# Decoder layer on one core: threshold steps with constants in PSUM, key and query transposes inside the last recurrence unit, two scans moved ahead of the attention

## Chip, core and metric

One Trainium2 chip, one core. The metric is the device time of one execution in microseconds (us), lower is better. TensorE is called PE, VectorE DVE, ScalarE ACT, GpSimd POOL, SyncE SP.

## What is computed

One layer of a hybrid decoder over 1024 prompt tokens and 8 decode tokens (1032 columns in all), width 1024, in fp32 accuracy (every matmul operand is split into a high and a low part). Of the reference, what matters here:

```
h   = modulate(rms_norm(x), shift, scale)
xr, gr, q, k, v, iq, ik, iw = split(h @ w_in)
xc  = causal_conv(xr);  r, gi = sigmoid(block products of xc)
a   = exp(-8 * softplus(-lambda) * r)
h_t = a_t * h_(t-1) + sqrt(1 - a_t^2) * gi_t * xc_t        (linear recurrence, 512 channels)
out_a = gelu(gr) * h
score = sum_heads iw * relu(iq . ik);  keep the 256 best keys of each query
out_b = softmax(q . k over the kept keys) @ v              (8 query heads, 2 key heads)
x = x + g1 * ([norm(out_a), norm(out_b)] @ w_out);  x = x + g2 * swiglu(...)
```

The 256 best keys are found without a sort: a search over the 32 bits of the score's float pattern gives each query its threshold (the 256th best score), then ties at the threshold are cut to the right number.

## The kernel before

The program is written by hand for each engine: every engine has its own instruction list and they meet at semaphores. Nothing is scheduled automatically; what stands first in an engine's list runs first. There are seven query groups with a search (`NSEL` = 7: six tiles of 128 prompt queries, with 384 to 1024 keys, and the 8 decode queries with 1025 keys).

**The search** runs 32 rounds. In each, DVE counts in four groups how many scores reach a candidate (L1974), ACT does the other three (L1282), and DVE sets the next bit (L2033). Candidates and bit constants lie in PSUM bank 7 (`raised`, `flips`, `limit`), so that the small steps of a round read one operand in PSUM. Meanwhile PE makes the projections and the units 0 to 5 of the recurrence inputs (`unit`, 72 matmuls of 344 columns each), and POOL rotates queries and keys, splits weights and runs the convolution.

**Behind the search** DVE finishes the last convolution group (`conv_last`, L2040) and then does the last threshold steps (L2065 to L2101): from the bit pattern found it makes the next larger pattern, counts once more for three groups (L1974), picks one of the two, and clears patterns near zero. All of these are operations on [128, 7] int32 tiles with a drain between dependent ones. Then come seven more counts, the number of ties to keep (L2110), and the tie steps of the first four groups (`ties(0)` to `ties(3)`, four operations each, L2122 to L1781). Between them stand the DVE parts of the recurrence gates: `gated(c)` (L2052), `root_input(c)`, `rooted(c)` (L2061) for its four channel groups c, and `ada_row_late` (L2007), which copies a row of modulation products out of PSUM.

**ACT** makes the gates: `gate_r`, `gate_i` (L1320, L1324), tanh, exp, square and `root` (L1335) for groups 0 and 1, then evacuates unit 6, waits for the semaphore `s_gx` to reach 5 (which is `rooted(1)`), and makes the gates of groups 2 and 3. **PE** makes `gate_products` (L2946) for each group into banks that ACT frees, then unit 7 (L2939 to L2941) into banks 0 to 2, which waits for ACT's seventh gate. Half-way through unit 7, `ada_columns_late` (L2924) and `ada_late` (L2918) make modulation products.

**The attention** then starts: `keys_turned(i)` (L2999, 16 matmuls) transposes two tiles of keys into PSUM bank 7 or 6, ACT and DVE split them into high and low (`keys_high` L1376, `keys_low` L2141); `q_transposed(n)` (L3009, 4 matmuls) does so for the queries of group n, from a stack that `q_high`, `q_low` (L1391, L2179) make. Its 16 groups n (8 tiles of queries times 2 key heads) go through a loop: `logits` on PE (L3022, L3023), `masked` on DVE (L2196), `exponential` on ACT (L1405), `scaled_probs` on DVE (L2207), `transposed` (L3032), `probs_out` on ACT (L1414) and `mixed` on PE (L3044). Logits and exponentials run two groups ahead (`AHEAD` = 2). The four `scan(c)` of the recurrence (L2165 to L2172) stand in DVE's list of this loop behind groups 3, 5, 7 and 9:

```
SCAN_AT = (3, 5, 7, 9)
                if n in SCAN_AT:
                    scan(SCAN_AT.index(n))
```

Behind the attention come the decode queries, the output projection and the feed-forward part.

## Time and profile before

| what | value |
|---|---|
| three runs | 1353.51 us median, 1352.86 to 1359.51 |
| profiled execution | 1357.33 us, its span 1355.5 us |
| busy share | PE 95%, PE weight load 86%, DVE 66%, ACT 50%, POOL 52% |
| chain that ended last | PE 65%, DVE 13%, SP queue 5%, ACT 4%, issue 4%, POOL queue 3% |
| mean granted PE clock | 0.970 of full |

Positions below are microseconds from the span's start. The search runs from 133 to 282, the last threshold steps from 291 to 308, unit 7 from 330 to 345, the attention from 345 to 509, and from about 570 PE works nearly without a gap to the end. A row of the timeline has start, duration, engine, line, operation, output<-inputs, shapes and count, and in brackets how long the engine had been idle and what released it. A chain row has start, duration, engine, what it writes and its line.

### The profile page before, as it was taken

Reading aid. Unit: us, or ns where it says so; the run is one execution under the profiler, and the core shown is the slowest. Engines: PE = TensorE matmul, PEld = TensorE weight load, DVE = VectorE, ACT = ScalarE, POOL = GpSimd, SP = SyncE. Lnnn points to the kernel's source line nnn. Section 1 sums busy time; section 2 is a strip of 40 time slices with the busy share of each in tenths; the row PEclk is TensorE's granted clock in tenths of the full one; section 3 lists DMA queues with packets and bytes.
Section 4 is the critical chain, followed back from the end, with each engine's and each line's share of the span. In section 5 each row is a group of like instructions: output and inputs, shape, how many; then the busy total and the mean of one; then the engine's idle time right before and its main releaser. Section 6 shows DMA issues by size and latency. Waiting matters only on the chain.

```text
span 1355.5 us, 25270 instructions
## 1 busy us (share of the span) xinstructions
PE 1289.2 (95%) x9473; PEld 1163.5 (86%) x9473; DVE 891.7 (66%) x1621; ACT 679.6 (50%) x1156; POOL 698.2 (52%) x439
## 2 busy tenths in 40 slices
PE   6889999999889998899999999999999999999998
PEld 4575998787746655699999999999999999999998
DVE  6766889888789844766895355554555544654495
ACT  5546978958767764545534333433433336311115
POOL 0331567990000000345578788887887867666730
PEclk9789999999789997999999999999999999999999
DMA  9622105443101114265522243343433457899733
GB/s 358 248 67 70 48 1 187 141 164 101 46 18 33 53 33 145 85 216 167 168 74 70 88 143 122 143 161 145 165 125 117 165 219 272 319 325 354 263 126 126
DMA packets 126058, 198.86 MB, mean 147 GB/s; under 512 B 16775, under 2 KB 100047, under 8 KB 115568
## 3 DMA queue, kind: packets, MB, share of 16 engines
q1 hardware_dynamic: 125936, 197.24, 42.0%
q8 instruction: 75, 1.23, 0.4%
q14 instruction: 47, 0.39, 0.1%
HBM read 144.07 MB, written 53.18 MB: 146 GB/s over the span
## 4 chain that ended last, share of the span: by engine, by line
PE 65%; DVE 13%; SPq 5%; ACT 4%; issue 4%; POOLq 3%; DVEq 3%; POOL 2%; ACTq 1%; DMA 0%
PE ps L3300 29%; PE ps L3320 14%; DVE junk L1974 2%; PE ps L3164 2%; PE ps L3044 2%; PE ps L3166 2%; PE ps L3165 2%; SPq L676 2%; PE ps L3032 1%; SPq L675 1%; DVE lg L2196 1%; PE ps L3097 1%; PE ps L3022 1%; SPq L670 1%; DVEq L2495 1%
## 5 line engine op out<-in xcount | busy, mean ns | idle before, releaser
L983 POOL TENSOR_TENSOR wL<-wraw,wH 128x1024 fp32r<-128x1024 f32 x28 | 69.5, 2484 | 297.0 <-ACT wH L1275 296.8
L3320 PE MATMUL ps<-input,down_H 128*128 128x258 f32 x1120 | 180.6, 283 | 1.5 <-DVE acc L2643 1.5
L3320 PEld LDWEIGHTS ps<-input,down_H 128*128 128x128 f32 x1120 | 154.5, 190 | 2.1 <-issue 1.1
L3300 PE MATMUL ps<-comb,opH 128*128 128x258 f32 x960 | 154.4, 283 | 0.0
L1106 POOL TENSOR_TENSOR opL<-wsum,opH 128x512 fp32r<-128x512 f32 x80 | 124.5, 1566 | 36.0 <-ACT opH L1604 32.8
L1604 ACT CAST opH<-wsum 128x512 fp32r<-128x512 f32 x80 | 49.6, 621 | 167.1 <-PE ps L3300 103.5
L3300 PEld LDWEIGHTS ps<-comb,opH 128*128 128x128 f32 x960 | 132.7, 190 | 0.0
L3300 PE MATMUL ps<-h2H,opH 128*128 128x258 f32 x640 | 129.0, 283 | 0.3 <-DVE h2L L2500 0.3
L3300 PE MATMUL ps<-h2H,opL 128*128 128x258 f32 x640 | 129.0, 283 | 0.0
L3300 PE MATMUL ps<-h2L,opH 128*128 128x258 f32 x640 | 128.6, 282 | 0.0
L2643 DVE TENSOR_TENSOR acc<-ps,acc 128x516 f32<-128x516 f32 x112 | 76.6, 694 | 62.2 <-PE ps L3320 61.7
L1282 ACT ACTIVATE junk<-score,keyX 128x896 bf16<-128x896 f32 (+2 forms) x96 | 106.0, 1106 | 18.5 <-DVE keyX L2033 14.0
L3320 PE MATMUL ps<-input,down_L 128*128 128x258 f32 x560 | 113.1, 283 | 0.0
L1106 POOL TENSOR_TENSOR opL<-raw,opH 128x512 fp32r<-128x512 f32 x60 | 94.1, 1569 | 33.5 <-ACT opH L1604 33.5
L1974 DVE TENSOR_SCALAR_CACHE_REDUCE junk<-score,keyX 128x384 bf16<-128x384 f32 (+5 forms) x138 | 106.3, 826 | 0.1
L3300 PEld LDWEIGHTS ps<-h2H,opH 128*128 128x128 f32 x640 | 99.3, 189 | 0.5 <-issue 0.5
L3300 PEld LDWEIGHTS ps<-h2L,opH 128*128 128x128 f32 x640 | 99.1, 189 | 0.0
L3300 PEld LDWEIGHTS ps<-h2H,opL 128*128 128x128 f32 x640 | 99.0, 189 | 0.0
L3300 PE MATMUL ps<-comb,opL 128*128 128x258 f32 x480 | 96.8, 283 | 0.0
L3320 PEld LDWEIGHTS ps<-input,down_L 128*128 128x128 f32 x560 | 86.7, 190 | 0.0
L2572 DVE TENSOR_TENSOR staged<-gf,staged 128x1032 fp32r<-128x1032 f32 x35 | 60.2, 1721 | 34.0 <-ACT staged L1636 34.0
L3300 PEld LDWEIGHTS ps<-comb,opL 128*128 128x128 f32 x480 | 74.2, 189 | 0.0
(506 smaller groups left out, 3518.9 us busy)
## 6 DMA issues: line engine op xcount, KB each, us to landing
down_inputs<-staged SPq DMA_DIRECT2D x35, 1032.0 KB, 4.5
input<-down_inputs SPq DMA_DIRECT2D x35, 1032.0 KB, 6.8
adb<-in_ada_w SPq DMA_DIRECT2D x8, 2048.0 KB, 8.4
wraw<-in_w_out SPq DMA_DIRECT2D x24, 512.0 KB, 4.5
raw<-in_w_gate SPq DMA_DIRECT2D x10, 1024.0 KB, 6.4
raw<-in_w_up SPq DMA_DIRECT2D x10, 1024.0 KB, 5.1
down_block<-in_w_down SPq DMA_DIRECT2D x5, 2048.0 KB, 10.9
x_feature_major<-x0T SPq DMA_DIRECT2D x1, 4128.0 KB, 12.0
```

Source lines behind the costliest of these rows:

```text
L676: sp.dma_start(ipg[b // 2][:, g, (b % 2) * HD:(b % 2 + 1) * HD], a["cache_ik"][0][bass.ds(page, 1), :, :].rearrange("a s d -> (a s) d")).t ...
L983: pool.tensor_tensor(lo[:], raw_[:], hi[:].bitcast(F32), ALU.subtract).then_inc(s_wL, 1)
L1106: pool.tensor_tensor(opL[g % OPS][:], operand(v, p), opH[g % OPS][:].bitcast(F32), ALU.subtract).then_inc(s_wL, 1)
L1282: ins = A(junk[0:m, off:off + w], score[0:m, off:off + w], ACT.Sign, scale=-1.0, bias=keyXs[r % 2][0:m, n:n + 1].bitcast(F32), accum_out=c ...
L1604: nc.scalar.copy(opH[g % OPS][:], operand(v, p)).then_inc(s_wH, 1)
L1974: V.tensor_scalar(junk[0:m, off:off + w], score[0:m, off:off + w], thr[0:m, n:n + 1].bitcast(F32), 0.0, op, ALU.add, accum_out=cnt[0:m, n: ...
L2572: V.tensor_tensor(stg[n % 2][:, :, 1, :], down_input(b, p), stg[n % 2][:, :, 0, :].bitcast(F32), ALU.subtract).then_inc(s_aL, 1)
L2643: V.tensor_tensor(two(acc[p][:, m, :]), ps[:, 2 * m:2 * m + 2, 0:HC], two(acc[p][:, m, :]), ALU.add).then_inc(s_dne, 1)
L3044: ins = mm(ps[par * HD:(par + 1) * HD, 6 + n % 2, 0:2 * P], value, heads[:, par], start=(k == 0), stop=(k == tile_of(n)))
L3164: mm(dst, wH[s][:, k, :], hi, start=(k == 0), stop=False)
L3300: ins = mm(ps[:, sum_bank(v, p) + h, 0:HC], weight[s][:, k, :], token[:, k, h * HC:(h + 1) * HC], start=begins, stop=ends, skip_group_chec ...
L3320: ins = mm(ps[:, 2 * m + h, 0:HC], weight[:, f, cc], tok[:, f, part, h * HC:(h + 1) * HC], start=(f == 0 and weight is hi and part == 0), ...
```

## The change

It has three parts.

1. **Constants in PSUM.** Nine int32 constants are set with `memset` and copied to bank 7 ahead of the search. The last threshold steps, which were `tensor_scalar` with immediates, become `tensor_tensor` whose second operand is such a constant, broadcast over the seven columns, or an intermediate kept in PSUM (`key_mask`, `key_carry`, `key_low`, `key_next`). `top_mask` and the XOR behind it become `pattern`. The seven counts then stand in one piece ahead of `gated(0)`.
2. **Attention transposes in unit 7.** `keys_turned(0)`, `(1)`, `(2)` and `q_transposed(0)` are issued between the feature blocks 4 to 7 of unit 7; `keys_turned(1)` writes bank 5 and `(3)` bank 6. ACT's `keys_high` and `q_high(0)` move ahead of `root(2)`.
3. **Two scans earlier.** `scan(0)` and `scan(1)` leave the attention loop and stand among the ties and gates; the loop keeps `scan(2)` behind group 5 and `scan(3)` behind group 9. `ties(1)` and `ties(2)` move ahead of `rooted(0)`.

The core of the diff:

```diff
 UNIT_BIT = (20, 22, 25, 28, 31, 32, 32, 32)
-SCAN_AT = (3, 5, 7, 9)
+SCAN_AT = {5: 2, 9: 3}
+KEY_BANK = (7, 5, 7, 6)
+F_TOPK = 0x43800000
+KEY_CONSTS = (31, 16, 1, 65535, -1, -2147483648, 0x7FFFFFFF, 1 << 23, F_TOPK)
...
+        key_mask, key_carry, key_low, key_next = [ps[:, 7, 320 + 8 * j:320 + 8 * j + NSEL].bitcast(I32) for j in range(4)]
...
-            root(2)
-            root(3)
...
-                if i == 0:
-                    act.wait_ge(s_qkr, 1)
-                else:
+                if i:
...
+            keys_high(0)
+            keys_high(1)
+            q_high(0)
+            root(2)
+            root(3)
+            keys_high(2)
+            q_evac(0)
             A(dsm[:, 7:8], consts[0:64, C_ONE:C_ONE + 1], ACT.Gelu_apprx_tanh)
-            act.wait_ge(s_un, NU_LRU)
-            q_high(0)
             unit_evac(7)
-            keys_high(0)
-            q_evac(0)
             q_evac(1)
-            keys_high(1)
+            keys_high(3)
             for g in range(GRP):
                 exponential(g)
-            keys_high(2)
             q_high(1)
             for g in range(GRP, AHEAD * GRP):
                 exponential(g)
-            keys_high(3)
             q_evac(AHEAD)
...
-            def top_mask(key):
-
-                V.tensor_scalar(keyM[:], key[:], 31, None, ALU.arith_shift_right)
+            def constant(value, n=NSEL):
+
+                at_ = 416 + KEY_CONSTS.index(value)
+                return ps[:, 7, at_:at_ + 1].bitcast(I32).to_broadcast([P, n])
+
+            def pattern(key):
+
+                V.tensor_tensor(keyM[:], key[:], constant(31), ALU.arith_shift_right)
+                V.tensor_tensor(keyN[:], key[:], constant(-1), ALU.bitwise_xor)
                 dve.drain()
-                V.tensor_scalar(keyM[:], keyM[:], -1, -2147483648, ALU.bitwise_xor, ALU.bitwise_or)
+                V.tensor_tensor(key_mask, keyM[:], constant(0x7FFFFFFF), ALU.bitwise_and)
                 dve.drain()
-
+                V.tensor_tensor(keyX[:], keyN[:], key_mask, ALU.bitwise_xor)
+                dve.drain()
+
+            for j, value in enumerate(KEY_CONSTS):
+                V.memset(kset[:, j:j + 1], value)
+            dve.drain()
+            V.tensor_copy(ps[:, 7, 416:416 + len(KEY_CONSTS)].bitcast(I32), kset[:])
             V.memset(negb[:], NEG)
...
-            V.tensor_scalar(keyM[:], keyX[:], 31, -2147483648, ALU.arith_shift_right, ALU.bitwise_or)
-            dve.drain()
-            V.tensor_tensor(keyK[:], keyX[:], keyM[:], ALU.bitwise_xor)
-            dve.drain()
-            V.tensor_scalar(keyL[:, 0, :], keyK[:], 65535, None, ALU.bitwise_and)
-            V.tensor_scalar(keyL[:, 1, :], keyK[:], 16, None, ALU.arith_shift_right)
-            dve.drain()
-            V.tensor_scalar(keyL[:, 0, :], keyL[:, 0, :], 1, None, ALU.add)
-            dve.drain()
-            V.tensor_scalar(keyN[:], keyL[:, 0, :], 16, None, ALU.arith_shift_right)
...
-            top_mask(keyC)
-            V.tensor_tensor(keyX[:], keyC[:], keyM[:], ALU.bitwise_xor)
-            dve.drain()
...
+            V.tensor_tensor(keyM[:], keyX[:], constant(31), ALU.arith_shift_right)
+            dve.drain()
+            V.tensor_tensor(key_mask, keyM[:], constant(-2147483648), ALU.bitwise_or)
+            dve.drain()
+            V.tensor_tensor(keyK[:], keyX[:], key_mask, ALU.bitwise_xor)
+            dve.drain()
+            V.tensor_tensor(keyL[:, 0, :], keyK[:], constant(65535), ALU.bitwise_and)
+            V.tensor_tensor(keyL[:, 1, :], keyK[:], constant(16), ALU.arith_shift_right)
+            dve.drain()
+            V.tensor_tensor(keyL[:, 0, :], keyL[:, 0, :], constant(1), ALU.add)
+            dve.drain()
+            V.tensor_tensor(key_carry, keyL[:, 0, :], constant(16), ALU.arith_shift_right)
+            V.tensor_tensor(key_low, keyL[:, 0, :], constant(65535), ALU.bitwise_and)
+            dve.drain()
+            V.tensor_tensor(keyL[:, 1, :], keyL[:, 1, :], key_carry, ALU.add)
+            dve.drain()
+            V.tensor_tensor(keyL[:, 1, :], keyL[:, 1, :], constant(16), ALU.logical_shift_left)
+            dve.drain()
+            V.tensor_tensor(keyC[:], keyL[:, 1, :], key_low, ALU.bitwise_or)
+            V.tensor_tensor(key_next, keyL[:, 1, :], key_low, ALU.bitwise_or)
+            dve.drain()
+            pattern(keyC)
             count(ALU.is_ge, keyX, SEL_ACT)
...
+            V.tensor_tensor(keep[:, SEL_ACT:], cnt[:, SEL_ACT:], constant(F_TOPK, NSEL - SEL_ACT).bitcast(F32), ALU.is_ge)
+            dve.drain()
+            V.copy_predicated(keyK[:, SEL_ACT:], keep[:, SEL_ACT:], key_next[:, SEL_ACT:])
+            dve.drain()
+            pattern(keyK)
+
+            V.tensor_tensor(keyN[:], keyX[:], constant(0x7FFFFFFF), ALU.bitwise_and)
+            V.memset(key_next, 0)
+            dve.drain()
+            V.tensor_tensor(keep[:], keyN[:], constant(1 << 23), ALU.is_lt)
+            dve.drain()
+            V.copy_predicated(keyX[:], keep[:], key_next)
             dve.drain()
             ada_row_late(ADA_1 + 5)
+            count(ALU.is_gt, keyX)
+            dve.drain()
+            V.tensor_scalar(cnt[:], cnt[:], -1.0, float(TOPK), ALU.mult, ALU.add)
+            dve.drain()
             gated(0)
-            count(ALU.is_gt, keyX, 0, SEL_ACT)
             gated(1)
-            count(ALU.is_gt, keyX, SEL_ACT)
-            dve.drain()
-
-            V.tensor_scalar(cnt[:], cnt[:], -1.0, float(TOPK), ALU.mult, ALU.add)
-            dve.drain()
-            root_input(0)
-            root_input(1)
...
-            ties(0)
-            rooted(0)
-            rooted(1)
-            ada_row_late(ADA_1 + 6)
-            ties(1)
-            gated(2)
-            gated(3)
-            ties(2)
-            root_input(2)
-            root_input(3)
-            ada_row_late(ADA_1 + 7)
-            ties(3)
...
+            ties(0)
+            ties(1)
+            root_input(0)
+            root_input(1)
+            ties(2)
+            rooted(0)
+            rooted(1)
+            ada_row_late(ADA_1 + 6)
+            dve.wait_ge(s_lev, 6)
+            scan(0)
+            gated(2)
+            gated(3)
+            ties(3)
+            root_input(2)
+            root_input(3)
+            ada_row_late(ADA_1 + 7)
+            keys_low(0)
+            keys_low(1)
             q_low(0)
-            keys_low(0)
+            scan(1)
+            keys_low(2)
             rooted(2)
...
-            keys_low(1)
+            keys_low(3)
             for g in range(GRP, AHEAD * GRP):
                 masked(g)
-            keys_low(2)
             q_low(1)
-            keys_low(3)
...
-                    scan(SCAN_AT.index(n))
+                    scan(SCAN_AT[n])
...
-                    if k == KH and between is not None:
-                        pe.wait_ge(s_gs, 2 * LT)
-                        ada_columns_late(between - 1, 3, 0)
-                        ada_late(between)
+                    if between is not None:
+                        between(k)
...
-            unit(7, hH, hL, 0, ADA_1 + 7)
 
             def keys_turned(i):
-                if i >= 2:
-                    pe.wait_ge(s_kl, i - 1)
+                if i == 2:
+                    pe.wait_ge(s_kl, 1)
...
-            pe.wait_ge(s_qkr, 1)
-            keys_turned(0)
+            def attention_begun(k):
+
+                if k == KH:
+                    pe.wait_ge(s_gs, 2 * LT)
+                    ada_columns_late(ADA - 2, 3, 0)
+                    ada_late(ADA - 1)
+                    pe.wait_ge(s_qkr, 1)
+                    keys_turned(0)
+                elif k == KH + 1:
+                    keys_turned(1)
+                elif k == KH + 2:
+                    keys_turned(2)
+                elif k == KD - 1:
+                    q_transposed(0)
+
+            unit(7, hH, hL, 0, attention_begun)
             ada_columns_late(ADA - 1, 6, 0)
-            pe.wait_ge(s_gs, 2 * LT)
-            q_transposed(0)
+            pe.wait_ge(s_kl, 2)
             q_transposed(1)
             pe.wait_ge(s_lmod, 1)
-            keys_turned(1)
+            keys_turned(3)
             pe.wait_ge(s_lev, NU_LRU)
-            pe.wait_ge(s_kl, 1)
-            for g in range(GRP):
+            for g in range(AHEAD * GRP):
                 logits(g)
-            keys_turned(2)
-            for g in range(GRP, AHEAD * GRP):
-                logits(g)
-            keys_turned(3)
             pe.wait_ge(s_kl, NTT // 2)```

What it does to DVE's list around the gates of groups 0 and 1 (spare and gel hold the gate terms, eqb and preb the tie terms, mrowb a modulation row; L1781 is the helper for three-operand steps, and L1783 in the new kernel). Before:

```order
L1781 SCALAR_TENSOR_TENSOR spare_174<-spare_173,spare_174 128x1032 [waits decay_squared]
L1781 SCALAR_TENSOR_TENSOR gel<-gel 128x1032 [waits decay_squared]
L2122 TENSOR_SCALAR eqb<-score,keyX 128x384
L2125 SCALAR_TENSOR_TENSOR preb<-eqb 128x384
L1781 SCALAR_TENSOR_TENSOR eqb<-preb,cnt,eqb 128x384
L1781 SCALAR_TENSOR_TENSOR score<-score,keyX,eqb 128x384
L2061 TENSOR_TENSOR xr<-xr,spare_174 128x1032 [waits lru_root]
L2061 TENSOR_TENSOR xr<-xr,gel 128x1032 [waits lru_root]
```

Now, in the same place:

```order
L1783 SCALAR_TENSOR_TENSOR spare_175<-spare_174,spare_175 128x1032 [waits decay_squared]
L1783 SCALAR_TENSOR_TENSOR gel<-gel 128x1032 [waits decay_squared]
L2131 TENSOR_SCALAR eqb<-score,keyX 128x640
L2134 SCALAR_TENSOR_TENSOR preb<-eqb 128x640
L1783 SCALAR_TENSOR_TENSOR eqb<-preb,cnt,eqb 128x640
L1783 SCALAR_TENSOR_TENSOR score<-score,keyX,eqb 128x640
L2075 TENSOR_TENSOR xr<-xr,spare_175 128x1032 [waits lru_root]
L2075 TENSOR_TENSOR xr<-xr,gel 128x1032 [waits lru_root]
L2021 COPY mrowb_148<-ps 128x256 [waits ada_columns,ada_product]
L2021 COPY mrowb_149<-ps 128x256
L2156 TENSOR_TENSOR decay_170<-decay_170,stT 128x8 [waits lru_evacuated]
L2157 SCALAR_TENSOR_TENSOR xr<-decay_170,xr 128x1024
```

The ties between the root inputs and the rooted products are now those of 640 keys; those of 384 and 512 keys stand ahead of the root inputs, and a scan follows the row copies.

On PE, behind unit 7, before (qk holds the keys to turn, stk the stacked queries):

```order
L2999 MATMUL ps<-consts,qk 64x128 [waits qk_rotated]
L2999 MATMUL ps<-consts,qk 64x128 x7
L2924 MATMUL ps<-consts,mrowb_147 128x9 [waits ada_row_evacuated]
L2924 MATMUL ps<-consts,mrowb_147 128x9
L2924 MATMUL ps<-consts,mrowb_148 128x9 x2
L3009 MATMUL ps<-consts,stk 128x128 [waits q_stack_low,gate_sigmoid]
L3009 MATMUL ps<-consts,stk 128x128 x3
L3009 MATMUL ps<-consts,stk 128x128 [waits q_stack_low]
L3009 MATMUL ps<-consts,stk 128x128 x3
L2999 MATMUL ps<-consts,qk 64x128 [waits late_modulation_ready]
L2999 MATMUL ps<-consts,qk 64x128 x7
L3022 MATMUL ps<-kT,qT 128x128 [waits bank_evacuated,k_low,lru_evacuated]
```

Now, from the end of unit 7 on:

```order
L2937 MATMUL ps<-consts,mrowb_148 128x9 [waits ada_row_evacuated]
L2937 MATMUL ps<-consts,mrowb_148 128x9
L2937 MATMUL ps<-consts,mrowb_149 128x9 x2
L3019 MATMUL ps<-consts,stk 128x128 [waits q_stack_low,k_low]
L3019 MATMUL ps<-consts,stk 128x128 x3
L3009 MATMUL ps<-consts,qk 64x128 [waits late_modulation_ready]
L3009 MATMUL ps<-consts,qk 64x128 x7
L3032 MATMUL ps<-kT,qT 128x128 [waits bank_evacuated,lru_evacuated]
```

One key transpose and one query transpose are left there; the others now stand inside unit 7, where the third of them waits for `k_low` and the query transpose for `q_stack_low`, both of which DVE gives.

## Rows read from the trace of the kernel before

**Rows 1.** The chain that ended last, 290 to 305 us: start, us, engine and what.
```profile
290.79 1.73 DVE keyM L2065
292.85 2.21 DVE keyL L2069
295.20 0.94 DVE keyL L2072
296.83 1.05 DVE keyL L2079
298.44 2.26 DVE keyM L1993
304.66 1.63 DVE keep L2088
```
**Rows 2.** Timeline of POOL over the same stretch.
```profile
290.06 2.43 POOL L1045 TENSOR_TENSOR gel<-gel 128x1032 f32<-128x1032 f32 x1 [0.15 <-issue]
...
295.01 2.84 POOL L1042 TENSOR_SCALAR gel<-xr,vec 128x1024 f32<-128x1024 f32 x1
...
298.29 2.38 POOL L1045 TENSOR_TENSOR gel<-gel 128x1032 f32<-128x1032 f32 x1
...
303.90 2.36 POOL L1051 TENSOR_TENSOR xr<-xr,gel 128x1032 f32<-128x1032 f32 x1
```
**Rows 3.** Timeline of DVE: a search step with PSUM operand, two later small steps.
```profile
278.16 0.16 DVE L1987 TENSOR_TENSOR keyX<-keyX,ps 128x7 int32<-128x7 int32 x1
...
297.95 0.17 DVE L2081 TENSOR_TENSOR keyC<-keyL 128x7 int32<-128x7 int32 x1
298.20 0.17 DVE L1991 TENSOR_SCALAR keyM<-keyC 128x7 int32<-128x7 int32 x1
```
**Rows 4.** The instructions of line 1926, the bit constants ahead of the search.
```profile
L1926 DVE MEMSET bits<- x31: 59/59/59, 73.2 to 75.2; 128x1 int32 x31
```
**Rows 5.** Timeline of DVE: the second rooted product.
```profile
324.75 1.23 DVE L2061 TENSOR_TENSOR xr<-xr,gel 128x1032 f32<-128x1032 f32 x1
```
**Rows 6.** Timeline of ACT: gate_i(1), and gate_r(2) behind its table load.
```profile
308.10 1.12 ACT L1324 ACTIVATE gel<-ps,vec 128x1032 f32<-128x1032 f32 x1 [0.62 <-PE ps L2946]
...
326.02 1.12 ACT L1320 ACTIVATE decay<-ps,vec 128x1032 f32<-128x1032 f32 x1
```
**Rows 7.** Stretches of ties(1), ties(2): length, busy of steps on score, clock.
```profile
326.77:330.33 3.56, 0.00 (x0) 0.00 (x0) 1.24 (x2) 0.00 (x0) 1.00 1.05 356
333.27:337.33 4.06, 0.00 (x0) 0.00 (x0) 1.43 (x2) 0.00 (x0) 1.00 0.02 4
```
**Rows 8.** Timeline of PE from unit 7's end to the first turned probabilities.
```profile
344.98 1.09 PE L2999 MATMUL ps<-consts,qk 128*64 128x128 f32 x16
...
353.35 1.98 PE L2999 MATMUL ps<-consts,qk 128*64 128x128 f32 x16
...
360.77 1.11 PE L3009 MATMUL ps<-consts,stk 128*128 128x128 f32 x4 [1.41 <-DVE kT L2141]
361.81 1.12 PE L3032 MATMUL ps<-consts,lg 128*128 128x128 f32 x4
```
**Rows 9.** The chain that ended last, at the first and third scan.
```profile
383.05 2.20 DVE xr L2166
...
387.06 1.15 DVE score L1781
...
419.72 2.20 DVE xr L2166
```
**Rows 10.** Timeline of PE behind the first scan.
```profile
389.47 0.50 PE L3022 MATMUL ps<-kT,qT 128*128 128x512 f32 x1 [2.12 <-DVE nb L2196]
```
**Rows 11.** Stretches: busy of PE, PE load, DVE, ACT, POOL; clock; DMA share; GB/s.
```profile
350.00:366.00 16.00, 14.27 (x82) 12.21 (x78) 9.83 (x43) 10.00 (x28) 0.00 (x0) 0.50 0.21 60
390.00:398.00 8.00, 7.13 (x25) 3.98 (x25) 6.26 (x18) 6.37 (x16) 0.00 (x0) 0.57 0.19 54
415.00:430.00 15.00, 13.05 (x86) 8.70 (x83) 14.53 (x32) 11.50 (x25) 0.00 (x0) 1.00 0.07 21
```

33 lines of the change are left out of this document (11 added, 22 removed).

## The prediction

> **What bounds the kernel now.** I read four views. The table of the page says that PE is busy 95% of the span and has 65% of the chain that ended last; DVE has 13% of it. From about 570 us to the end PE works nearly without a gap, so whatever lets the attention end earlier should bring the end forward by as much. The question is therefore which waits between 282 and 509 us the change takes from the chain, and the rest of the reading stays there.
>
> The chain [rows 1] shows six of DVE's last threshold steps with 0.94 to 2.26 us each, all on [128, 7] tiles. Small steps of the same shape take 0.17 us and start 0.25 us after one another when each waits for the one before [rows 3] (the two from 297.95 on). The timeline of POOL [rows 2] says what the long ones have in common: the first ends at 290.79 + 1.73 = 292.52, as POOL's step of 290.06 ends (292.49); the second ends at 295.06, where POOL's next but one starts (295.01); the fourth at 297.88, with POOL's scalar step (297.85); the fifth at 300.70, with 298.29 + 2.38 = 300.67; the sixth at 306.29, with 303.90 + 2.36 = 306.26. DVE waits for POOL in them. The Trainium skill, SBUF — State Buffer, "Who interferes with whom", says that a DVE instruction in a mode that uses both port pairs, or one with two SBUF inputs against a POOL step that reads SBUF, is blocked for POOL's whole instruction, and that one with a single SBUF input outside those modes is not; by that rule, which these five ends fit, the new steps would never wait.
>
> In the attention loop the chain runs through the scans [rows 9]; PE waits 2.12 us for DVE behind the first [rows 10], and the granted clock is 0.57 of full in the 8 us from 390 on, so mostly at 1.2 instead of 2.4 GHz [rows 11]. Around the third scan PE is busy 13.05 of 15 us and DVE 14.53 of 15 [rows 11].
>
> **The change part by part.**
>
> *Constants.* Nine memsets and a copy are added ahead of the search. The 62 memsets that alternate from 73.2 to 75.2 [rows 4] start 0.03 us apart and last 0.06, so nine are 0.3 to 0.5 us, and the copy behind a drain is one step of 0.25. Every engine's work follows the search's rounds there, so I take it in full: **+0.6** (0 to +0.8).
>
> *Threshold steps.* The six long ones sum to 9.82 us; at 0.17 each they would be 1.02, so 8.8 go. The new list has one more dependent step (0.25) and three more second halves of a pair (about 0.08 each), 0.5 in all: 8.3 us less. This assumes 0.16 us for a `tensor_tensor` with a PSUM operand, which the search shows 31 times on the same shape [rows 3] (278.16). The Trainium skill, VectorE: DVE Perf Modes, "The TRN2 errata", speaks against that: it gives 120 cycles of fixed cost for a PSUM source against 58 for SBUF at 0.96 GHz, which is an estimate of 65 ns more for each of some 25 steps, 1.6 us, and would make the forecast 1347.2. The row at 278.16 (PSUM) is not longer than the one at 297.95 (SBUF), so the measurement decides for 0.16.
>
> *Order before unit 7.* ACT's gates of groups 2 and 3 wait for `rooted(1)`, which ended at 324.75 + 1.23 = 325.98 [rows 5], and ACT went on at 326.02 [rows 6]; PE's unit 7 follows from them. Ahead of that point DVE now has `ties(1)` and `ties(2)` too, 3.56 and 4.06 us [rows 7], and `gated(1)`, behind all counts, may wait for ACT's gate, which ends at 308.10 + 1.12 = 309.2 [rows 6]; I reckon 0.4. So -8.3 + 3.56 + 4.06 + 0.4 = -0.3: all that the threshold steps give is spent on ties. An earlier `rooted(1)` brings little, since ACT has a table load right ahead of 326.02. Unit 7 starts as before: **0** (-0.3 to +1.1, if both `gated` steps wait).
>
> *Start of the attention.* Up to the loop DVE's list has two scans more (8.4, below) and 8.3 less, so DVE reaches its first `masked` as before. PE has the same transposes, but two of the 16-matmul groups that cost 1.98 at the low clock [rows 8] (353.35) are issued inside unit 7, where such a group takes 1.09 (344.98): 1.8 less; and the wait of 1.41 for the last keys at 360.77 [rows 8] should go, since `keys_low(2)` and `(3)` are earlier. If DVE alone sets the start, nothing is gained; if PE does, 3.2. Walking both lists with these durations I get the first turned probabilities at 359.8 instead of 361.81: **-2.0** (-3.2 to 0). What is late next there is DVE's `s_lmod`, for which PE's last key transpose waits behind `scan(1)` and `keys_low(2)`.
>
> Inside unit 7 PE can now block: `keys_turned(2)` waits for `keys_low(0)`, `q_transposed(0)` for `q_low(0)`, and 18 and 9 matmuls of unit 7 stand behind them. My walk has about 1.5 us of slack at both, so I cost the waits at nothing; that cover goes if DVE is later than that.
>
> *First scan out of the loop.* It begins one small step (0.17) before the chain's row of 383.05, and the next work starts at 387.06 [rows 9]: 4.2 us in which DVE gives nothing to PE and ACT. Below stands PE's recorded wait of 2.1 [rows 10]; above, 4.2 plus what the low clock costs in the 8 us from 390 (PE 7.13 busy at 0.57 [rows 11]), some 2 more that PE would not need. I take the scan and a little of the clock: **-4.5** (-6 to -2.1).
>
> *The scan behind group 7* (419.7 [rows 9]) is the second place that gets none; groups 5 and 9 keep theirs. Here the clock is full, and PE idles only 15 - 13.05 = 1.95 us [rows 11], so PE takes over as the bound once DVE is 4.2 shorter: **-2.0** (-4.2 to 0).
>
> The SP queue loads key pages of the decode queries behind `scan(0)` and `scan(1)`; these now go out earlier, and nothing waits for them before the loop ends. POOL is idle from 306.3 on. Both nothing.
>
> Sum: 0.6 - 2.0 - 4.5 - 2.0 = **-7.9**. Against the profiled execution's own 1357.33 us (span 1355.5, 1.8 outside it) that is 1349.4; this execution lies 3.8 above the median of the three runs, so against the median it is 1353.5 - 7.9 = **1345.6 us**.
>
> **The rivals.**
>
> *The loop is PE's already.* PE and ACT have enough other work in the loop, and the removed scans pay only what PE was seen to wait: 2.1, and 0.5 for the second. For it speaks PE's 13.05 of 15 us; against it the low clock behind the first scan, which a PE that is the bound would not show. -2.6 - 2.0 + 0.6 = -4.0: 1349.5.
>
> *The long steps are first uses, not waits for POOL.* Each long step of rows 1 uses an operation that DVE has not run before in that form, and a repetition is short. Then the new list pays again: it has nine pairs of operation and place (shift, and, or, add, left shift, less-than, with output in SBUF or PSUM) that the search does not run, each at the mean excess of 8.8 / 6 = 1.47, so 13.2 us. That delay reaches `rooted(1)`, unit 7 and the attention at once, less 0.3 of slack: 1345.6 + 12.9 = 1358.5, slower by 5.0. It decides against the change from 7.9 + 0.3 = 8.2 us on, some six of the nine. Against it: five ends agree with POOL's to 0.05 us, and the first `or` of two tensors, at 297.95, takes 0.17 [rows 3].
>
> *PE keeps its clock at the start.* From 350 to 366 us PE is busy 14.27 of 16 us at half clock [rows 11]. With the transposes inside unit 7, less idle time stands ahead of the logits; if the clock then does not fall, PE's 14.27 would be about 7.1, and ACT (10.0) and DVE (9.83) set the pace. Of the 6 us between I give it half, 3: 1342.6. Against it: PE still waits for DVE between unit 7 and the logits, as it did when the clock fell.
>
> **How the numbers follow.** Forecast 0.60, PE's loop 0.25, clock 0.09, first uses 0.06. All bounds of the terms at once give -13.5 and -0.2; the forecast's own range is 1341.5 to 1350, and with the rivals 1341.5 to 1351.5 leaves out no more than 2 in 10. A measurement of this kernel can tell about 0.5% from no change, 6.8 us: faster is under 1346.7, slower over 1360.3. The forecast lies under 1346.7 in four of five of its cases (0.48), the clock rival in all (0.09), PE's loop in few (0.03): 0.60. Slower takes the dearest first uses: 0.03. The rest, 0.37, is within.
>
> **What would show it.** In the profile of the changed kernel: the steps between `conv_last` and the seven counts have no row over 0.3 us beside POOL's rows and take about 9 us with three counts, not 17; if rows of 1 to 2 us stand there and end where no POOL row ends, the second rival holds. `rooted(1)` ends within 1 us of 326.6 (the old time plus 0.6) and unit 7 starts as late behind it as before. PE shows no wait for `kT` or `stk` inside unit 7. The first turned probabilities come near 360.4. There is one scan between 380 and 425 us, no stretch at half clock near 390, and the loop's 147 us (361.8 to 509) are about 140.5. The forecast is wrong if that loop is over 144 us (the first rival), or if PE idles inside unit 7.

## The result and the profile after

The changed kernel takes 1349.39 us in the median of 13 runs (1346.16 to 1354.34), the kernel before, in runs beside it, 1356.87 (1352.86 to 1361.23). The ratio is 0.9949, 95% interval 0.9937 to 0.9962: 6.9 us less (5.2 to 8.5), at the edge of the 0.5% that was called no change. The forecast was -7.9 with a range of -12.0 to -2.0, against 1353.5 us, the median of three earlier runs of the kernel before; the 1345.6 us that it named goes with that figure, so the differences are compared and not the times. The profiled execution of the changed kernel took 1351.9 us, span 1350.1.

Of the page's busy table and of its chain, after:

```profile
PE 1284.1 (95%) x9473; PEld 1161.0 (86%) x9473; DVE 882.8 (65%) x1635; ACT 679.3 (50%) x1156; POOL 698.7 (52%) x439
PE 71%; DVE 11%; SPq 5%; issue 3%; ACT 3%; DVEq 2%; POOLq 2%; POOL 1%; DMA 1%; ACTq 0%
```

DVE's share of the chain fell from 13 to 11%, PE's rose from 65 to 71%.

The two profiled executions are not aligned: the search ends (start of its last COPY_PREDICATED) at 281.80 us before and at 286.67 after. So I compare stretches, not positions. The modulation columns in unit 7 are PE's step half-way through that unit (`ada_columns_late`); the first turned probabilities are PE's first `transposed` step.

| stretch, us | before | after | change |
|---|---|---|---|
| start to end of the search | 281.80 | 286.67 | +4.87, of it 0.44 the constants |
| end of the search to the modulation columns in unit 7 | 54.61 | 54.21 | -0.40 |
| from there to the first turned probabilities | 25.40 | 21.75 | -3.65 |
| the attention loop, to PE's first step of the decode queries | 147.40 | 141.28 | -6.12 |
| from there to the end of the span | 846.3 | 846.2 | -0.1 |

The threshold steps, timeline of DVE after, to be held against [rows 1]:

```profile
295.33 0.16 DVE L2079 TENSOR_TENSOR keyM<-keyX,ps 128x7 int32<-128x7 int32 x1
...
298.10 0.17 DVE L2001 TENSOR_TENSOR ps<-keyM,ps 128x7 int32<-128x7 int32 x1
...
302.22 0.16 DVE L2103 TENSOR_TENSOR keep<-cnt,ps 128x3 int32<-128x3 f32 x1
...
304.33 0.76 DVE L2021 COPY mrowb<-ps 128x256 f32<-128x256 f32 x2
```

POOL's timeline beside them:

```profile
294.60 2.41 POOL L1050 TENSOR_TENSOR gel<-gel 128x1032 f32<-128x1032 f32 x1 [0.15 <-issue]
297.16 2.41 POOL L988 TENSOR_TENSOR lL<-lraw,lH 128x1024 fp32r<-128x1024 f32 x1
```

POOL works as before, and no small step is longer than 0.17 us. The block lasts 304.33 - 295.33 = 9.00 us, against 308.15 - 290.79 = 17.36 before.

What the saved time became stands in three timelines, of DVE, ACT and PE, after:

```profile
329.21 1.24 DVE L2075 TENSOR_TENSOR xr<-xr,gel 128x1032 f32<-128x1032 f32 x1
```
```profile
330.48 1.12 ACT L1325 ACTIVATE decay<-ps,vec 128x1032 f32<-128x1032 f32 x1 [0.80 <-DVE xr L2075]
```
```profile
331.65 3.74 PE L2957 MATMUL ps<-xr,wbd 128*128 128x344 f32 x12 [1.59 <-ACT decay L1325]
```

`rooted(1)` ends 43.8 us behind the search's end (330.45 - 286.67), where it ended 44.2 behind it [rows 5]. ACT could have gone on 0.80 us sooner.

The start of the attention, timeline of PE after, against [rows 8]:

```profile
343.61 1.09 PE L3009 MATMUL ps<-consts,qk 128*64 128x128 f32 x16
...
348.90 1.09 PE L3009 MATMUL ps<-consts,qk 128*64 128x128 f32 x16
...
351.46 0.60 PE L3019 MATMUL ps<-consts,stk 128*128 128x128 f32 x4
...
355.61 1.09 PE L3009 MATMUL ps<-consts,qk 128*64 128x128 f32 x16 [0.84 <-DVEq L2233]
356.63 0.33 PE L3032 MATMUL ps<-kT,qT 128*128 128x128 f32 x1
...
361.63 1.09 PE L3019 MATMUL ps<-consts,stk 128*128 128x128 f32 x4 [1.26 <-issue]
362.63 1.11 PE L3042 MATMUL ps<-consts,lg 128*128 128x128 f32 x4
```

Nothing inside unit 7 waits. Three key transposes and one query transpose that stood behind it are now in it at full clock, and the next thing late is DVE's `s_lmod` (L2233), 0.84 us. The query transpose ahead of the first turned probabilities, which waited 1.41 us for keys before, still waits 1.26, now for DVE's `q_low`, which ends at 360.84 + 0.69 = 361.53:

```profile
360.84 0.69 DVE L2170 TENSOR_TENSOR stk<-qk,stk 128x512 fp32r<-128x512 f32 x1
```

The stretch from the modulation columns to the first turned probabilities, before and after (columns as in [rows 11]):

```profile
336.41:361.81 25.40, 22.48 (x163) 18.45 (x161) 18.37 (x42) 19.09 (x39) 0.00 (x0) 0.76 0.12 35
340.88:362.63 21.75, 18.52 (x163) 14.88 (x161) 18.04 (x45) 18.66 (x39) 0.00 (x0) 0.96 0.07 20
```

PE has the same 163 matmuls there. They keep it busy 3.96 us less, at a mean clock of 0.96 instead of 0.76, and it waits 3.23 us (21.75 - 18.52) where it waited 2.92 (25.40 - 22.48). So all of the 3.65 us, and a little more, is work done at a higher clock; the waits did not get shorter.

Stretches after: length, busy of PE, PE load, DVE, ACT, POOL; clock; DMA share; GB/s, to be held against [rows 11]:

```profile
350.00:361.00 11.00, 8.41 (x66) 7.44 (x66) 9.36 (x29) 10.62 (x24) 0.00 (x0) 1.00 0.11 32
361.00:366.00 5.00, 4.37 (x20) 4.03 (x21) 3.21 (x16) 3.62 (x14) 0.00 (x0) 0.50 0.23 66
...
390.00:398.00 8.00, 6.44 (x40) 4.18 (x40) 6.47 (x18) 6.68 (x17) 0.00 (x0) 1.00 0.20 58
...
415.00:430.00 15.00, 13.96 (x92) 9.15 (x92) 11.14 (x25) 12.31 (x25) 0.00 (x0) 1.00 0.01 2
```

Before, PE was at half clock from 350 to 366; now it is so only from 361. The half-clock stretch near 390 is gone. Around 415 to 430 PE's busy time rose from 13.05 to 13.96 of 15 and DVE's fell from 14.53 to 11.14.

### The profile page after: what moved, and what is told of

It is laid out like the page before. It is cut to its first block, busy times and chain, and to the rows that moved or that the text cites. A ratio compares the mean times of both kernels' runs of the same rounds, so it can differ in the third digit from the quotient of the medians.

```text
span 1350.1 us, 25285 instructions
## 1 busy us (share of the span) xinstructions
PE 1284.1 (95%) x9473; PEld 1161.0 (86%) x9473; DVE 882.8 (65%) x1635; ACT 679.3 (50%) x1156; POOL 698.7 (52%) x439
## 3 DMA queue, kind: packets, MB, share of 16 engines
q8 instruction: 75, 1.23, 0.4%
## 4 chain that ended last, share of the span: by engine, by line
PE 71%; DVE 11%; SPq 5%; issue 3%; ACT 3%; DVEq 2%; POOLq 2%; POOL 1%; DMA 1%; ACTq 0%
PE ps L3318 29%; PE ps L3338 14%; PE ps L3054 2%; PE ps L3182 2%; PE ps L3183 2%; PE ps L3184 2%; SPq L681 2%; PE ps L2919 2%; PE ps L2921 2%; PE ps L3042 2%; PE ps L2920 1%; SPq L680 1%; DVE lg L2187 1%; PE ps L3115 1%; SPq L675 1%
## 5 line engine op out<-in xcount | busy, mean ns | idle before, releaser
L988 POOL TENSOR_TENSOR wL<-wraw,wH 128x1024 fp32r<-128x1024 f32 x28 | 69.5, 2485 | 286.9 <-ACT wH L1280 286.8
```

The source lines that it names most:

```text
L988: pool.tensor_tensor(lo[:], raw_[:], hi[:].bitcast(F32), ALU.subtract).then_inc(s_wL, 1)
```

## The experiments

All times are against the kernel before in the same session, from the ratio of medians times 1356.9 us, with the 95% interval. The other columns are read from one profiled execution of each kernel, with the marks of above: where the search ends, from there to the modulation columns in unit 7 and to the first turned probabilities, and the length of the loop. Single executions scatter: the four whose scans stand behind 3, 5, 7 and 9 (before, constants only, all scans back, forms warmed) have loops of 145.73 to 147.40 us, and the kernel before and the one with forms warmed, which has the same loop, differ by 1.67. In that pair the clock from 388 to 396 us is 0.66 and 0.79. The four with the changed kernel's two scans (changed, immediates, SBUF constants, ties(2) behind) lie closer, 141.18 to 141.55. A difference of 1 to 2 us between two loops below is therefore a reading of two executions and no more.

| kernel | time, us | ratio | search ends | to unit 7 | to attention | loop |
|---|---|---|---|---|---|---|
| before | 0 | 1 | 281.80 | 54.61 | 80.01 | 147.40 |
| changed | -6.9 (-8.5 to -5.2) | 0.9949 | 286.67 | 54.21 | 75.96 | 141.28 |
| constants only | -2.0 (-3.9 to -0.1) | 0.9985 | 281.41 | 53.47 | 77.50 | 146.95 |
| all scans back | -3.0 (-4.7 to -1.1) | 0.9978 | 283.15 | 53.61 | 75.04 | 147.02 |
| scan(1) behind 3 | -4.3 (-6.2 to -2.3) | 0.9968 | 286.96 | 54.24 | 75.66 | 145.10 |
| scan(1) behind 7 | -8.3 (-10.6 to -6.1) | 0.9939 | 285.19 | 53.60 | 75.02 | 142.64 |
| immediates | +1.1 (-0.5 to +2.7) | 1.0008 | 282.02 | 62.72 | 84.48 | 141.55 |
| SBUF constants | -4.3 (-6.2 to -2.6) | 0.9968 | 282.35 | 57.83 | 79.59 | 141.26 |
| scans behind 9, 12 | +7.6 (+5.2 to +9.9) | 1.0056 | 282.29 | 54.45 | 76.56 | 143.68 |
| scans behind 7, 10, 12 | +7.5 (+5.0 to +9.9) | 1.0055 | 283.04 | 54.21 | 75.63 | 144.55 |
| tie step moved | -5.8 (-7.9 to -3.8) | 0.9957 | 284.81 | 53.60 | 75.02 | 143.93 |
| scans behind 5, 7 | -9.1 (-11.3 to -6.9) | 0.9933 | 284.99 | 54.28 | 76.03 | 140.66 |
| ties(2) behind | -7.6 (-10.0 to -5.3) | 0.9944 | 281.27 | 53.57 | 75.34 | 141.18 |
| forms warmed | +1.2 (-0.5 to +3.0) | 1.0009 | 283.81 | 54.28 | 79.67 | 145.73 |

### The first part alone

The kernel before, with `keyM` to `keyX` as in the changed kernel's diff, the constants and `pattern`, but `gated`, counts, `ties`, scans and transposes where they were:

```diff
-            V.tensor_scalar(keyM[:], keyX[:], 31, -2147483648, ALU.arith_shift_right, ALU.bitwise_or)
+            V.tensor_tensor(keyM[:], keyX[:], constant(31), ALU.arith_shift_right)
+            dve.drain()
+            V.tensor_tensor(key_mask, keyM[:], constant(-2147483648), ALU.bitwise_or)
...
```

> The kernel before with the first part alone: constants and intermediates in PSUM, the order of all lists as before. Port theory (the long steps waited for POOL): no step over 0.3 us between the last convolution group and the seven counts, that stretch 8.3 us shorter; but ahead of unit 7 DVE was waited for only once, 0.92 us at ACT's first root, so unit 7 starts about 0.9 us earlier relative to the end of the search and the rest of the 8.3 becomes idle time of DVE; at the attention's start the wait of 1.4 us for the last keys may go too. Time: 0.6 - 0.9 - (0 to 1.4), 1 to 2 us under the kernel before, within what can be told from no change. First-use theory: long steps stay, slower by 0 to 5 us. If the whole 8.3 us were on the path, the time would fall by 7 to 8 us.

Measured -2.0 us. Unit 7's columns come 1.14 us sooner, the attention 2.51. The 0.92 us that ACT waited for DVE's root input is in ACT's timeline of before:

```profile
319.39 1.06 ACT L1335 ACTIVATE spare<-spare 128x1032 f32<-128x1032 f32 x1 [0.92 <-DVE spare L1781]
```

So 8.4 us off DVE's list, with nothing put in their place, are worth about a quarter of that. From the search's end to unit 7's columns ACT of this run has no wait for DVE over 0.15 us left, only waits for PE, so the chain of ACT's gates and PE's products sets the pace there. The wait for the last keys at the attention's start, which I thought might go, stays at 1.41 us. The 1.37 us gained behind the columns (24.03 against 25.40) come with a clock of 0.87 instead of 0.76: PE is busy 20.06 us instead of 22.48 and waits 3.97 instead of 2.92.

### The scans

Three kernels from the changed one: all four back in the loop, `scan(1)` alone back behind group 3, and the same behind group 7.

```diff
-SCAN_AT = {5: 2, 9: 3}
+SCAN_AT = {3: 0, 5: 1, 7: 2, 9: 3}
...
-            dve.wait_ge(s_lev, 6)
-            scan(0)
...
-            scan(1)
```
```diff
-SCAN_AT = {5: 2, 9: 3}
+SCAN_AT = {3: 1, 5: 2, 9: 3}
...
-            scan(1)
```
```diff
-SCAN_AT = {5: 2, 9: 3}
+SCAN_AT = {5: 1, 7: 2, 9: 3}
...
-            scan(1)
```

> The changed kernel with all four scans back in the attention loop behind groups 3, 5, 7 and 9 (parts 1 and 2 stay). Theory of the prediction: the two scans pay 6.5 us in the loop, so the time is 6 to 7 us over the changed kernel, less what DVE gains ahead of the attention without them (at most 1 to 2 us, since DVE is waited for there 0.84 us by the last key transpose): 4.5 to 6.5 us over it, and the clock falls again behind the first scan. Rival (the loop is PE's already): 2.6 us in the loop and the start earlier by 1 to 2, so 0.5 to 2 us over the changed kernel.

> The changed kernel with scan(1) back in the loop behind group 3; scans behind 5 and 9 stay. Theory: place 3 costs 4.5 us (2.1 if only PE's recorded wait counts), with a stretch at about half clock near 390 us; the start of the attention is up to 0.8 us earlier. So 1.3 to 4.5 us over the changed kernel, 3.7 likeliest.

> The changed kernel with scan(1) back in the loop behind group 7; scans behind 5 and 9 stay. Theory: place 7 costs 2.0 us (0 to 4.2) at full clock, the start of the attention is up to 0.8 us earlier: 1.2 us over the changed kernel, and less than with place 3. If every scan in the loop costs its 4.2 us wherever it stands, this one and the run with place 3 come out alike, 3.4 us over.

Measured -3.0, -4.3 and -8.3 us, so 3.9 and 2.6 over and 1.4 under the changed kernel by the medians. Only the first is apart from the changed kernel beyond the intervals (0.9965 to 0.9992 against 0.9937 to 0.9962); it is less than the 4.5 to 6.5 expected, and the third has the other sign than the 1.2 over that was expected. The loops go with the places: 147.02 with all four, 142.64 without place 3 (4.4 less), 141.28 without 7 too (1.4 less), and 145.10 with 3 but not 7 (3.8 over the changed kernel). The difference can be dated: `attT` of the fourth group (L2204) is copied 27.5 us behind the first turned probabilities with the scan at 3 and 23.3 without, and the gap stays to the loop's end. Both differences of the loop are near the forecast's 4.5 and 2.0, the second within the scatter of single executions. From 388 to 396 us the clock was 0.69 with the scan at 3 (all four back) and 1.00 without it (scan(1) behind 7). That the time with all scans back is 3.9 and not 6 to 7 over is in small part the start: the attention begins 0.92 us sooner (75.04 against 75.96). The run with scan(0) ahead and scan(1) not has 75.02, so scan(0) is free there. Of the 0.94 between that run and the changed kernel only 0.33 can be scan(1)'s: 0.61 lie ahead of the columns in unit 7 (53.60 against 54.21), where both lists are the same, and where `gated(1)` waits 0.45 us for ACT in the changed kernel's profile and not in the other. From the columns on it is 21.42 or 21.43 us in all five runs with scan(1) in the loop, and 21.75 to 21.77 in five of the six with it ahead (22.11 with scans behind 9 and 12). PE's timeline with scan(1) behind 7 shows what it held up:

```profile
352.61 1.09 PE L3008 MATMUL ps<-consts,qk 128*64 128x128 f32 x16
```

The last key transpose has no wait for `s_lmod` left; the query transpose behind the logits waits longer instead (1.93 us against 1.26), so little is gained. By the profiles `scan(1)` ahead of the attention costs 0.3 us and behind group 7 it costs 1.4; the times don't tell the two kernels apart (0.9922 to 0.9955 against 0.9937 to 0.9962).

### The immediates back

The changed kernel with the threshold steps of before, all else as changed (the `constant` and `pattern` of the diff reversed):

```diff
-            V.tensor_tensor(keyM[:], keyX[:], constant(31), ALU.arith_shift_right)
+            V.tensor_scalar(keyM[:], keyX[:], 31, -2147483648, ALU.arith_shift_right, ALU.bitwise_or)
...
```

> The changed kernel with the threshold steps of before again (immediates, no PSUM operands); the order of the lists, with ties(1) and ties(2) ahead of the rooted products, stays. Theory (port waits, and the 8.3 us were spent on the order ahead of unit 7): six or so steps of 1 to 2.3 us come back, that stretch is 17 us again, and now all of it reaches rooted(1), ACT's gates, unit 7 and the attention, less 0.8 us of slack at ACT: 7 to 8 us over the changed kernel, about as slow as or slower than before. If the saved 8.3 us had been idle time, the run would be within 1 us of the changed kernel.

Measured +1.1 us, 8.0 over the changed kernel; unit 7 and the attention start 8.5 us later, the loop is as long (141.55). The whole 8.4 us arrive. So the constants are worth 2 us in the old order and 8 in the new one, where two ties stand in the time they freed. ACT waits for DVE in this run at `gated(0)`, at the first root input and at `rooted(1)`:

```profile
317.33 1.07 ACT L1336 ACTIVATE spare<-decay 128x1032 f32<-128x1032 f32 x1 [3.52 <-DVE xr L2054]
...
326.15 1.06 ACT L1340 ACTIVATE spare<-spare 128x1032 f32<-128x1032 f32 x1 [5.30 <-DVE spare L1783]
...
333.99 1.12 ACT L1325 ACTIVATE decay<-ps,vec 128x1032 f32<-128x1032 f32 x1 [1.23 <-DVE xr L2063]
```

The changed kernel has only the third of these waits, 0.80 us.

### Why the steps were long

Two kernels. The changed one with its constants read from SBUF (the tile `psum_r` is unused there until the attention):

```diff
-                at_ = 416 + KEY_CONSTS.index(value)
-                return ps[:, 7, at_:at_ + 1].bitcast(I32).to_broadcast([P, n])
+                at_ = KEY_CONSTS.index(value)
+                return kset[:, at_:at_ + 1].to_broadcast([P, n])
...
+        kset = psum_r[:, 0:len(KEY_CONSTS)].bitcast(I32)
```

And the kernel before with the forms run once ahead of the search:

```diff
+            V.memset(keyC[:], 1)
+            dve.drain()
+            V.tensor_scalar(keyM[:], keyC[:], 31, -2147483648, ALU.arith_shift_right, ALU.bitwise_or)
+            V.tensor_scalar(keyL[:, 0, :], keyC[:], 65535, None, ALU.bitwise_and)
+            V.tensor_scalar(keyL[:, 1, :], keyC[:], 16, None, ALU.arith_shift_right)
...
```

> The changed kernel with the nine constants read from SBUF instead of PSUM, the same tensor_tensor steps otherwise; so some ten of them have two SBUF inputs while POOL works. Port theory: steps of 0.5 to 2.5 us appear in the threshold stretch and end where a row of POOL ends; the stretch is 12 to 18 us, the time 3 to 8 us over the changed kernel. If two SBUF inputs don't wait for POOL (only the immediates' form did), the stretch stays at 9 us and the time within 1 us of the changed kernel. First-use theory says nothing about the operand's place: 9 us too, since none of these steps was long in the changed kernel.

> The kernel before with the immediates' forms of the threshold steps run once on unused tiles ahead of the search (shift with or, and, shift, add, left shift, xor with or, less-than). Port theory: the six long steps stay as long as they were (0.9 to 2.3 us) and end where POOL's rows end; the time is up to 0.8 us over the kernel before. First-use theory: the forms are known by then, all steps of the stretch take 0.2 us, and the stretch is 8.8 us shorter.

Timelines of DVE and POOL with SBUF constants:

```profile
291.00 1.71 DVE L2079 TENSOR_TENSOR keyM<-keyX,psum_r 128x7 int32<-128x7 int32 x1
...
293.29 1.97 DVE L2085 TENSOR_TENSOR keyL<-keyK,psum_r 128x7 int32<-128x7 int32 x1
...
295.44 0.90 DVE L2088 CUSTOM_DVE_ANT_0 keyL<-psum_r,keyL 128x14 uint16<-128x14 uint16 x1
...
302.02 0.17 DVE L2103 TENSOR_TENSOR keep<-cnt,psum_r 128x3 int32<-128x3 f32 x1
...
303.31 0.17 DVE L2109 TENSOR_TENSOR keyN<-keyX,psum_r 128x7 int32<-128x7 int32 x1
```
```profile
290.27 2.42 POOL L1050 TENSOR_TENSOR gel<-gel 128x1032 f32<-128x1032 f32 x1 [0.15 <-issue]
292.84 2.40 POOL L988 TENSOR_TENSOR lL<-lraw,lH 128x1024 fp32r<-128x1024 f32 x1
295.21 2.85 POOL L1047 TENSOR_SCALAR gel<-xr,vec 128x1024 f32<-128x1024 f32 x1
...
301.06 2.91 POOL L1054 TENSOR_SCALAR xr<-xr,vec 128x1032 f32<-128x1032 f32 x1 [0.17 <-issue]
```

The first ends at 292.71, POOL's step at 292.69; the second at 295.26, POOL's at 295.24. One change of the second operand's place, PSUM to SBUF, turns 0.16 us into 1.71 and 1.97 in the same instruction. The stretch, up to the row copy at 304.17, is 13.17 us, 4.2 over the changed kernel's. The time is 2.6 over it, less than the 3 to 8 expected and with intervals that overlap (0.9954 to 0.9981 against 0.9937 to 0.9962). So what decides is whether the second operand lies in SBUF while POOL works; the form with immediates is not needed for the wait. The Trainium skill, SBUF — State Buffer, "Who interferes with whom", says that a DVE instruction with two SBUF inputs contends with a POOL instruction that reads SBUF. These two rows agree; those at 302.02 and 303.31, 0.17 us inside POOL's scalar step of 301.06 to 303.97, do not, nor do three more with two SBUF inputs during it and five during the one of 295.21, and the measurement decides: here tensor_tensor waited for POOL's tensor_tensor to its end, and during POOL's scalar steps it was long only once, 0.90 us at 295.44, with no end of POOL's there.

With the forms warmed, DVE and POOL:

```profile
292.42 1.72 DVE L2079 TENSOR_SCALAR keyM<-keyX 128x7 int32<-128x7 int32 x1
...
300.07 2.27 DVE L1993 TENSOR_SCALAR keyM<-keyM 128x7 int32<-128x7 int32 x1
```
```profile
291.69 2.42 POOL L1045 TENSOR_TENSOR gel<-gel 128x1032 f32<-128x1032 f32 x1 [0.15 <-issue]
...
299.92 2.39 POOL L1045 TENSOR_TENSOR gel<-gel 128x1032 f32<-128x1032 f32 x1
```

All six are as long as before to 0.01 us (1.72, 2.21, 0.94, 1.05, 2.27, 1.64), and the two shown end with POOL's rows (294.14 and 294.11; 302.34 and 302.31). The forms of the first five had run ahead of the search, 0.16 to 0.17 us each; that of the sixth, a comparison of counts, had not. For the five, first use has nothing to do with it; the sixth rests on its end alone, which agrees with POOL's to 0.03 us in the kernel before (306.29 and 306.26).

### Later places for the scans

DVE was busy 43 of the 50 us from 380 to 430 in the changed kernel (the expectation below has 45, misread), but only 50 of 79 from 430 on, so I tried the late groups:

```diff
-SCAN_AT = {5: 2, 9: 3}
+SCAN_AT = {9: 2, 12: 3}
```
```diff
-SCAN_AT = {5: 2, 9: 3}
+SCAN_AT = {7: 1, 10: 2, 12: 3}
...
-            scan(1)
```

> The changed kernel with the two scans that stay in the loop behind groups 9 and 12 instead of 5 and 9. In its trace DVE is busy 45 of the 50 us from 380 to 430 but only 50 of the 79 from 430 to 509. Theory that a scan costs by how full DVE is where it stands: the place behind group 5 costs 1 to 3 us, the late ones nothing, so 1 to 3 us under the changed kernel. Against: if the loop is PE's by then, within 0.5 us; if the last scan delays the key pages of the decode queries (the SP queue loads two of them behind the fourth scan), the decode stage grows instead.

> The changed kernel with scan(0) ahead of unit 7 as it is and the other three in the loop behind groups 7, 10 and 12. With scan(1) behind group 7 the time was 1.4 us under the changed kernel (start 0.9 us earlier, loop 1.4 us longer in the profiles). If a scan costs by how full DVE is where it stands, taking the place behind group 5 away too gives 2 to 4 us under the changed kernel in all. If not, 1 to 2.

Both misses: +7.6 and +7.5 us over the kernel before, 14.5 over the changed one. Two causes can be seen. The loop became 2.4 and 3.3 us longer instead of shorter. And the decode stage waits; SP, ACT and PE with scans behind 9 and 12:

```profile
538.71 2.57 SPq L714 DMA_DIRECT2D wraw<-in_w_out  x3
```
```profile
542.78 1.04 ACT L1280 CAST wH<-wraw 128x1024 fp32r<-128x1024 f32 x1 [8.15 <-DMA wraw<-in_w_out]
```
```profile
544.88 1.97 PE L3148 MATMUL ps<-consts,kpg 128*128 128x128 f32 x8 [6.66 <-ACT kbT L1464]
```

SP in the changed kernel:

```profile
525.86 2.47 SPq L714 DMA_DIRECT2D wraw<-in_w_out  x3
```

SP loads the key pages of two decode queries only when the fourth scan is done, then 48 value pages (52.9 us of its queue here), then these weights. The weights are asked for 12.9 us later, and ACT and PE wait for them. From the loop's end to the end of the span it is 7.8 and 9.6 us more. (With scans behind 9 and 12 the profile so shows 0.6 + 2.4 + 7.8 = 10.8 of the 14.5; that profiled execution lay 3.8 under its kernel's median, and the changed kernel's 2.5 over its own.) I had named the key pages as what could be late; it is the weights two places behind them in the same queue.

The loop taught the second thing. Per place, from the loops of these runs (a scan more or less, differences of the positions at which each group's `attT` is copied): 3.8 to 4.4 us behind group 3, 1.2 behind 5, 1.4 behind 7, about 2 behind 9, 3.0 behind 10, 2.1 and 3.6 behind 12 in the two runs. Behind 3, 10 and 12 a tie step stands behind the scan in the same group, behind 5, 7 and 9 none (`TIE_AT`). Each of these prices comes from one or two pairs of single executions.

### A tie step away from the scan

```diff
-SCAN_AT = {5: 2, 9: 3}
+SCAN_AT = {3: 1, 5: 2, 9: 3}
...
-TIE_AT = ((0, 1, 2, 3), (4, 6, 8, 10), (11, 12, 13, 14))
+TIE_AT = ((0, 1, 2, 4), (4, 6, 8, 10), (11, 12, 13, 14))
...
-            scan(1)
```

> The run with scan(1) behind group 3, with the last tie step of the fifth group moved from group 3 to group 4, where the scan no longer stands ahead of it (the number of steps is the same; group 4 now has two). In the runs so far a scan cost 3.8 to 4.3 us behind group 3, 3.0 behind 10, about 3.5 behind 12, where a tie step follows it in the same group, and 1.2 to 2.3 behind 5, 7 and 9, where none does. Theory of the collision (DVE can't serve PE for scan and tie step together, 4.2 + 1.2 us): the loop, 145.1 us with the scan at 3, falls by 1.5 to 2.5 us; the time is 1.5 to 2.5 us under that run, 0 to 1 us over the changed kernel. Rival (a scan there costs by itself, through the clock that falls behind it): the loop stays at 145 and the time at 2.6 us over the changed kernel.

Timeline of DVE with scan and tie step both behind 3:

```profile
386.62 1.23 DVE L2163 TENSOR_TENSOR gel<-gel,xr 128x1032 f32<-128x1032 f32 x1
387.97 1.15 DVE L1783 SCALAR_TENSOR_TENSOR score<-score,keyX,late_eq 128x896 f32<-128x896 f32 x1
...
389.63 0.69 DVE L2187 CUSTOM_DVE_ANT_0 lg<-ps,score 128x512 f32<-128x512 f32 x1 [0.21 <-issue]
```

With the tie step moved:

```profile
383.70 1.23 DVE L2163 TENSOR_TENSOR gel<-gel,xr 128x1032 f32<-128x1032 f32 x1
...
385.43 0.69 DVE L2187 CUSTOM_DVE_ANT_0 lg<-ps,score 128x512 f32<-128x512 f32 x1 [0.20 <-PE ps L3018]
```

PE behind the scan, first as it was, then with the step moved:

```profile
390.38 0.50 PE L3031 MATMUL ps<-kT,qT 128*128 128x512 f32 x1 [2.11 <-DVE nb L2187]
```
```profile
386.18 0.50 PE L3031 MATMUL ps<-kT,qT 128*128 128x512 f32 x1 [0.84 <-DVE nb L2187]
```

The next masked logits come 5.75 us behind the scan's beginning (389.63 - 383.88) and 4.48 with the step moved (385.43 - 380.95); PE's wait falls from 2.11 to 0.84; the loop from 145.10 to 143.93. That is 1.2 of the 1.5 to 2.5 us expected, about the tie step's own 1.15 and no more. The time is 1.5 us under that run's, with intervals that overlap. The loop is still 2.65 over the changed kernel's, more than the 1.2 to 2 of the other free places. So the collision can be seen in the rows, and is about a third of the price of place 3. Between 380 and 395 us the clock was 0.89 of full in this run and 1.00 in the changed kernel; how much of the rest is the clock and how much the place, the runs don't tell.

### The fourth scan behind group 7

```diff
-SCAN_AT = {5: 2, 9: 3}
+SCAN_AT = {5: 2, 7: 3}
```

> The changed kernel with its fourth scan behind group 7 instead of 9. Places 7 and 9 both have no tie step; they cost 1.4 and about 2 us in the loops so far. Theory: 0.3 to 1 us under the changed kernel, not to be told from it; the last key pages of the decode queries are loaded 20 us earlier, and nothing waits for them, so the decode stage stays as it is. If its waits are shorter, that stage was waiting for those pages after all.

Measured -9.1 us, 1348.11 in the median of 6; the loop is 0.62 us shorter and the decode stage as long. It is the fastest by point, but its interval (0.9917 to 0.9949) touches the changed kernel's (0.9937 to 0.9962), so it can't be called faster than it.

### Ties behind rooted(1)

```diff
-            ties(2)
             rooted(0)
             rooted(1)
             ada_row_late(ADA_1 + 6)
+            ties(2)
```

> The changed kernel with ties(2), 4.1 us, moved back behind rooted(1). Theory: ACT waited 0.80 us for rooted(1), so unit 7 starts 0.8 us earlier and no more (ACT's table load and PE's 1.6 us wait stand right behind it); DVE has as much to do up to the attention, and waited 1.2 us there, so the attention's start is 0 to 0.8 us earlier. Time 0 to 1 us under the changed kernel. If rooted(1) were the only thing ahead of unit 7, 4 us.

Measured -7.6 us (-10.0 to -5.3), the same as the changed kernel. Unit 7 lies 0.64 us sooner behind the search and the attention 0.62; but unit 7 lies as early in three runs whose list is the changed kernel's up to there (53.60 and 53.61), so even that is not shown to be the tie's. What is shown is that 4.1 us moved off the way to `rooted(1)` give no 4 us.

## Why the prediction was right

**Constants, +0.6.** From the memset of `keyX` to the copy of the bits it is 0.69 us (137.13 to 137.82) against 0.25 (132.81 to 133.06): +0.44. Right.

**Threshold steps, -8.3.** 17.36 to 9.00: -8.36. Right, and the reason with it: with the second input in SBUF long steps return, two of which end with POOL's, and warmed forms are as long as cold ones. The 65 ns more per step that the Trainium skill, VectorE: DVE Perf Modes, "The TRN2 errata", gives for PSUM sources are not there: the steps with a PSUM input take 0.15 to 0.17 us.

**Order before unit 7, 0.** -0.40 measured. Right in size and reason; the immediates put back show the other side of it, +8.5 there and +8.0 in the time. The 0.4 for `gated(1)` came too: it waited 0.45 us for ACT's gate. What I didn't see is that before, too, ACT had waited for DVE only 0.92 us ahead of unit 7, so that the 8.3 us would have brought little there and were free to be spent on ties.

**Start of the attention, -2.0, bounds -3.2 to 0.** This is the term that was wrong, in size and in mechanism: -3.65. I counted two transposes at a lower price and one wait that should go. The wait did not go: 1.41 us for keys became 1.26 for `q_low`, and all waits of PE in the stretch are 3.23 us against 2.92. The two transposes were misread as well. Of the three groups now inside unit 7 only one had cost 1.98 us before, the others 1.68 and 1.09; the second of 1.98 is the last one, which stays outside and takes 1.09 now (355.61). The four take 4.36 us instead of 6.73, so 2.4 less. The rest of the 3.96 us that PE is busy less stands mostly in the logits, which I had priced as they were, at half clock. That the clock holds was my rival with 0.09, and it is what happened: full to 361 where it was half from 350 on. With the first part alone the stretch behind the columns loses 1.37, with all scans back 3.97 (21.43), and the changed kernel gives 0.3 of that back for scan(1). Why the clock held is not shown apart: the runs change order and transposes together.

**First scan out, -4.5.** 4.4 by one pair of loops, 3.8 by the other. Right in size. The 4.2 us were too few, though: the row at 387.06, which I took for the next work, is the tie step itself, and DVE gives PE its next masked logits only at 388.72, 5.75 us behind the scan's beginning at 382.97. About a third of the price is that step.

**Second scan, -2.0.** 1.4. Right in kind. The loop went to 141.28 where 140.5 was forecast and 144 would have been wrong, and the first rival (PE's loop, 2.6 us for both scans) falls: the two are worth 5.7 in the loop (147.02 - 141.28). That the single price is 1.4 and not 1 or 2, one pair of executions can't say.

**The sum.** By the profiles, +0.44 - 0.40 - 3.65 - 6.12 = -9.7. The medians say -6.9, at most -8.5. So the terms gave 1.8 more than forecast and the total 1.0 less: that the total is so near -7.9 is partly luck, for the start's 1.65 too few was made up by something that no term covers. (All bounds at once are -13.7 to -0.2, not -13.5.) Of the 2.8 us between profiles and medians (1.2 at the interval's end) some may be the loop: by the means of the four loops of each kind it is 146.8 to 141.3, -5.5 and not -6.12. The rest must stand ahead of the search's end, where the two profiles differ by 4.43 us beyond the constants and the change adds only these. Timeline of PE before and after, where it waits for index key pages:

```profile
78.53 1.97 PE L2830 MATMUL ps<-consts,ipg 128*128 128x128 f32 x8 [3.59 <-DMA ipg<-in_cache_ik]
```
```profile
78.64 1.97 PE L2843 MATMUL ps<-consts,ipg 128*128 128x128 f32 x8 [5.65 <-DMA ipg<-in_cache_ik]
```

And the stretch behind it, before and after (columns as in [rows 11]):

```profile
84.00:110.00 26.00, 23.26 (x138) 17.72 (x137) 13.82 (x34) 13.30 (x25) 8.39 (x16) 1.00 0.13 30
```
```profile
84.00:110.00 26.00, 23.86 (x126) 18.58 (x124) 11.94 (x31) 10.98 (x22) 6.93 (x15) 0.86 0.13 30
```

The last pages land at the same time (86.40 and 86.48 us); in the profiled execution after, PE came to them 2 us sooner, waited 2 us longer, and had a clock of 0.86 behind it instead of 1.00. DVE's copy of the last scores, right ahead of the search, starts at 131.59 and 135.90, so 4.31 us are there before the search begins. This part varies from execution to execution: in the 14 profiles the search ends between 281.3 and 287.0 us. The kernel before and the two built on it lie at 281.8, 281.4 and 283.8 (this one with 1.4 us of warmed forms ahead), the eleven with the changed order at 281.3 to 287.0, in the mean 283.9. Whether the changed program, its 0.44 for constants taken off, really is some 1.7 us later there, or these are draws from the same spread, stays open; I found nothing in the change that touches that stretch, and no run was made for it.

## What to carry to other kernels

A DVE step on a tiny tile that takes microseconds is worth a look at POOL's timeline: if it ends where POOL's step ends, moving its second input to PSUM can take the wait away, as it did here (17.36 to 9.00 us). Where a stretch got shorter, split it into busy time and waits before naming the cause: the start of the attention gained 3.65 us with no less waiting. Time taken off an engine that is seldom waited for is worth little by itself (2 of 8.4 us here) and must be spent: something that is in the way elsewhere is moved into it. A filler that is placed between groups of a pipelined loop is priced by its place, by what stands next to it in the same gap (1.2 to 4.4 us for the same scan) and by the queue of another engine that waits for its semaphore, several transfers further on (8 to 10 us in the decode stage).

## What the runs showed of the hardware that was not expected

Steps with two SBUF inputs waited for POOL's tensor_tensor to its end, but ran in 0.17 us during its scalar step of 2.91 us. The forms with immediates are as uneven before: inside the scalar step of 295.01 to 297.85 two ran in 0.16 and 0.17 us, and the left shift behind them took 1.05 and ended with it (297.88). One addition without a PSUM input took 0.90 to 0.94 us and ended 1.13 us into a POOL scalar step (296.34 behind 295.21 with SBUF constants, 296.14 behind 295.01 before), with no end of POOL's there; its cause is open. In the 14 profiles PE's clock behind a wait of 3 to 6 us for the same transfer was anywhere from 0.85 to 1.00 of full over the next 26 us, and with it the start of all that follows.
